# Two of four output-projection pieces multiplied in float32 instead of as rounded parts, and one expert load issued earlier

## The reference, cut to what matters

```python
def _token_mixer(x, w_in, ..., w_out):
    p = _split_columns(x @ w_in)
    ...
    o = jnp.concatenate([o_fox.reshape(B, T, -1), o_nsa.reshape(B, T, -1),
                         o_dsa.reshape(B, T, -1)], axis=-1)
    return o @ w_out            # 1024 x 1024

for l in range(DEPTH):
    mix = _token_mixer(x, ...)
    x = _layer_norm(ALPHA * x + mix, ln1_g[l], ln1_b[l])
    ffn = _moe(x, ...)          # 64 experts, 8 chosen for each token
    x = _layer_norm(ALPHA * x + ffn, ln2_g[l], ln2_b[l])
```

## Time and profile before

| | |
|---|---|
| runs of the kernel before | 1230.63, 1230.74, 1232.79 us; median 1230.74 |
| profiled execution | span 1229.1 us; no other time is recorded for it, so what lies around the span is taken as the distance to the median, 1.6 us |
| PE busy | 1203.0 us (98%) |
| DVE, ACT, POOL busy | 561.5, 347.1, 127.6 us |
| DMA | 454.90 MB, mean 370 GB/s |

### The profile page before, as it was taken

How to read it: one execution, slowest core, us unless ns; L and a number is a source line. 1 busy time by engine, 2 the same in 40 slices (tenths; PEclk the granted TensorE clock), 3 DMA queues, 4 the chain that set the end, 5 groups by cost and what they waited for, 6 DMA issues and landing times.

```text
span 1229.1 us, 25332 instructions
## 1 busy us (share of the span) xinstructions
PE 1203.0 (98%) x10411; PEld 625.6 (51%) x10413; DVE 561.5 (46%) x1554; ACT 347.1 (28%) x717; POOL 127.6 (10%) x173
## 2 busy tenths in 40 slices
PE   9999999999999999999999999999999999999995
PEld 8886843344344343433398868344334443443341
DVE  5888653333333333333388877433333333333334
ACT  5667411111111111111275673111111111111111
POOL 2662200000000000000045431000000000000000
PEclk9999999999999999999999999999999999999999
DMA  9544899999999999999945529999999999999994
GB/s 362 198 175 182 331 408 427 426 426 426 426 427 424 429 426 426 425 427 426 377 168 196 221 106 409 406 427 426 426 428 426 425 427 425 427 426 426 425 428 188
DMA packets 43289, 454.90 MB, mean 370 GB/s; under 512 B 5296, under 2 KB 6064, under 8 KB 8880
## 3 DMA queue, kind: packets, MB, share of 16 engines
q1 hardware_dynamic: 42608, 452.29, 88.5%
q10 hardware_dynamic: 576, 1.05, 0.2%
HBM read 452.27 MB, written 1.05 MB: 369 GB/s over the span
## 4 chain that ended last, share of the span: by engine, by line
PE 79%; DVE 9%; DMA 7%; ACT 3%; issue 1%; POOL 1%; ACTq 0%; DVEq 0%; POOLq 0%
PE banks L1105 34%; PE banks L1132 17%; PE banks L1078 7%; DMA expert_weights<-in_moe_w 5%; PE banks L1143 5%; PE banks L1118 2%; PE banks L1022 1%; PE banks L969 1%; DVE prob L1783 1%; PE banks L1059 1%; PE banks L971 1%; PE banks L970 1%; ACT prob L1380 1%; ACT piece_hi L1307 1%; PE banks L671 1%
## 5 line engine op out<-in xcount | busy, mean ns | idle before, releaser
L1105 PE MATMUL banks<-expert_weights,gathered 128*64 128x512 f32 x1520 | 340.3, 595 | 1.7 <-DMA expert_weights<-in_moe_w 1.7
L1105 PEld LDWEIGHTS banks<-expert_weights,gathered 128*64 128x64 f32 x1520 | 105.2, 137 | 230.0 <-issue 230.0
L1132 PE MATMUL banks<-expert_weights,hT 128*32 128x512 f32 x1600 | 182.0, 595 | 2.3 <-DVE gathered L1972 2.3
L1987 DVE TENSOR_TENSOR sig<-sig,banks 128x256 f32<-128x256 f32 (+1 forms) x66 | 27.2, 413 | 340.9 <-ACT sig L1497 340.9
L1510 ACT ACTIVATE y_hi<-banks,gate_slot 128x512 fp32r<-128x512 f32 x126 | 86.6, 687 | 289.9 <-PE banks L1132 289.9
L1997 DVE SCALAR_TENSOR_TENSOR y_lo<-banks,gate_slot,y_hi 128x512 fp32r<-128x512 f32 x126 | 94.6, 751 | 160.6 <-ACT y_hi L1510 160.6
L1497 ACT ACTIVATE sig<-banks 128x256 f32<-128x256 f32 x64 | 24.6, 384 | 409.9 <-PE banks L1105 409.9
L1078 PEld LDWEIGHTS banks<-hot,x_part 128*128 128x128 bf16 x3072 | 93.3, 98 | 50.3 <-issue 50.3
L1132 PEld LDWEIGHTS banks<-expert_weights,hT 128*32 128x32 f32 x1600 | 47.6, 109 | 108.9 <-issue 108.1
L1078 PE MATMUL banks<-hot,x_part 128*128 128x64 bf16 x3072 | 100.7, 193 | 0.0
L1569 POOL TENSOR_TENSOR piece_lo<-pieces,piece_hi 128x256 fp32r<-128x256 f32 x112 | 90.7, 847 | 72.4 <-ACT piece_hi L1307 58.7
(11 more groups left out here) (262 smaller groups left out, 1527.3 us busy)
## 6 DMA issues: line engine op xcount, KB each, us to landing
expert_weights<-in_moe_w SPq DMA_DIRECT2D x132, 2048.0 KB, 24.2
expert_weights_in_ring<-in_moe_w SPq DMA_DIRECT2D x20, 2048.0 KB, 23.8
pieces<-in_pieces SPq DMA_DIRECT2D x32, 1024.0 KB, 5.8
expert_weights<-in_moe_w SPq DMA_DIRECT2D x26, 1024.0 KB, 9.5
expert_weights_in_rows<-in_moe_w SPq DMA_DIRECT2D x22, 1024.0 KB, 23.1
expert_weights_in_x<-in_moe_w SPq DMA_DIRECT2D x22, 1024.0 KB, 23.9
expert_weights_in_ring<-in_moe_w SPq DMA_DIRECT2D x8, 1024.0 KB, 9.7
shared_weights<-in_ws SPq DMA_DIRECT2D x2, 3072.0 KB, 12.2
```

The costliest lines, as they stand in the source:

```text
L1105: mm = pe.matmul(C[e * PAIR:(e + 1) * PAIR, :], xgT[:, d, e * PAIR:(e + 1) * PAIR], w[e][:, part], start=(d == 0), stop=(d == KD - 1))
L1132: mm = pe.matmul((A, B)[c][to:to + SLOTS, :], hT[:, f, of_:of_ + SLOTS], W[QUARTERS + c][e][:, f * 512:(f + 1) * 512], start=(f == 0), sto ...
```

## The change

Pieces 2 and 3 of the output projection are no longer split. `SPLIT` loses them, so ACT drops three casts and DVE four subtractions a layer. PE multiplies them as float32 weights straight from the ring with float32 activations `xT`, one product in place of three, and waits for `o_sb` (the heads copied to `xT`) where it waited for `heads_split` (their parts made by POOL). Since the `hi` slots of pieces 2 and 3 are then free after the last input projection, load 5 is issued there; at `mix` 3, when nothing reads `x_hi`, `x_lo` and the parts any more, SP now issues both first quarters, load 4 and load 6.

```diff
-SPLIT_OUT = [n for n, (what, c) in enumerate(STREAM) if what == "out"]
+OUT_AT = [n for n, (what, c) in enumerate(STREAM) if what == "out"]
+SPLIT_OUT, WHOLE_OUT = OUT_AT[:2], OUT_AT[2:]
...
-LO_VECTOR = (1, 2, 3, 6, 14, 15, 16)
+LO_VECTOR = (1, 2, 3, 6, 14)
...
                     sp.wait_ge(*at(proj, 2 * N_IN_PIECES))
                     load_half(3, 0)
+                    load(5)
...
                     sp.wait_ge(*at(mix, 2 * TT - 1))
-                    load_first_quarter(0)
+                    for e in range(2):
+                        load_first_quarter(e)
                     load(4)
+                    load(6)
                     sp.wait_ge(*at(mix, 2 * TT))
-                    load_first_quarter(1)
                     load_half(3, 1)
-                    load(5)
-                    load(6)
...
+                        if c == 1:
+                            whole = pair_of(WHOLE_OUT[0], ring)
+                            for k in ks:
+                                mm = pe.matmul(out_, xT[:, k, cols], whole[:, :, k, :], start=(k == 0), stop=(k == KD - 1), skip_group_check=True)
+                            return mm
...
-                        pe.wait_ge(*at(heads_split, k + 1))
+                        if c == 0:
+                            pe.wait_ge(*at(heads_split, k + 1))
...
+                        else:
+                            pe.wait_ge(*at(o_sb, k + 1))
...
-                    split_hi(SPLIT_OUT[2])
...
-                    split_last_hi(0)
...
-                        if v == 6:
-                            split_last_hi(1)
...
-                        if 5 <= u < 9:
-                            split_out(2 + (u - 5) // 2, (u - 5) % 2)
-                        if u in (6, 8):
-                            own.settle()
-                            dve.nop().then_inc(lo_dve, 1)
```

More of the change, by code:

```diff
@@ L37 @@
 LAST_IN_SLOT = STREAM.index(("in", 10)) % RING
-assert LAST_IN_SLOT not in [n % RING for n in SPLIT_OUT]
-LO_VECTOR = (1, 2, 3, 6, 14, 15, 16)
+assert LAST_IN_SLOT not in [n % RING for n in OUT_AT]
+LO_VECTOR = (1, 2, 3, 6, 14)
 LO_POOL = [n for n in SPLIT if n not in LO_VECTOR]
@@ L394, in hi_free, with pair_of @@
                 eng.wait_ge(*at(proj, 2 * c + 2))
-        def lo_pair(n):
+        def pair_of(n, slots):
             a, b = sorted((PLACE_IN_RING[n % RING], PLACE_IN_RING[(n + 1) % RING]))
             assert a == PLACE_IN_RING[n % RING]
-            return lo_ring[:, a:b + 1:b - a]
+            return slots[:, a:b + 1:b - a]
         def flat_piece(t):
@@ L964, in out_product @@
                         cols = slice(t * P, (t + 1) * P)
-                        first = SPLIT_OUT[2 * c]
-                        hi, lo = hi_ring[:, hi_slot(first):hi_slot(first) + 2], lo_pair(first)
                         out_ = mixed_out(t, c).rearrange("p (n c) -> p n c", n=2)
+                        if c == 1:
[3 more added lines that the diff above has]
+                            return mm
+                        hi, lo = hi_ring[:, hi_slot(SPLIT_OUT[0]):hi_slot(SPLIT_OUT[0]) + 2], pair_of(SPLIT_OUT[0], lo_ring)
                         for k in ks:
@@ L975, in out_early @@
                     def out_early(c, k):
-                        pe.wait_ge(*at(heads_split, k + 1))
-                        if k == 0:
-                            for n in (2 * c, 2 * c + 1):
-                                parts_ready(pe, SPLIT_OUT[n])
+                        if c == 0:
+                            pe.wait_ge(*at(heads_split, k + 1))
+                            if k == 0:
+                                for n in SPLIT_OUT:
+                                    parts_ready(pe, n)
+                        else:
+                            pe.wait_ge(*at(o_sb, k + 1))
+                            if k == 0:
+                                for n in WHOLE_OUT:
+                                    pe.wait_ge(*at(piece_ld[n % RING], piece_count(n)))
                         return out_product(0, c, (k,))
@@ L1307, in split_hi @@
                             act.copy(flat_piece(hi_of(n))[:, cols], flat_piece(piece[n % RING])[:, cols]).then_inc(hi_ready, 1)
[L1309 to L1314, removed]
-                            own.settle()
-                            act.nop().then_inc(hi_ready, 1)
                     def columns_out(g):
@@ L1834, in cmp_norm @@
                         V.tensor_tensor(rows_, rows_, pcs[:, 2, :].unsqueeze(2).broadcast_to([P, TT * heads, NC]), ALU.mult).then_inc(pc_ready, 1)
-                    def split_out(i, half):
-                        n, cols = SPLIT_OUT[i], slice(half * SLOT // 8, (half + 1) * SLOT // 8)
-                        dve.wait_ge(*at(hi_ready, SPLIT.index(n) + 2))
-                        own.mark(V.tensor_tensor(flat_piece(piece_lo[n % RING])[:, cols], flat_piece(piece[n % RING])[:, cols],
-                                                 flat_piece(hi_of(n)).bitcast(F32)[:, cols], ALU.subtract))
                     normalise(2)
```

1 line of the change is left out of this document (removed).

## The result

| | before | after |
|---|---|---|
| median of 20 runs each (lowest to highest), us | 1230.59 (1228.74 to 1232.79) | 1233.16 (1231.52 to 1234.97) |
| ratio after / before, 95% interval | | 1.0023 [1.0017, 1.0029]: 2.8 us slower, 2.1 to 3.6 |
| span of the profiled execution, us | 1229.1 | 1232.7 |
| PE busy, us | 1203.0 | 1208.0 |
| DVE, ACT, POOL busy, us | 561.5, 347.1, 127.6 | 552.2, 339.2, 122.4 |

The change costs 2.8 us. The forecast was 1230.4 us and no change that can be measured. The rows show first what came as forecast.

The account below looks back on a forecast made before the run. PE and the chains feeding it were taken as the bound, weight waits costing only 3.5 us. Products (+2.9) less stalls (-1.3) shift PE 1.6 us a layer, mostly swallowed: -0.3 us together, 1230.4 us, range 1228.2 to 1233.4.

Parts of the forecast that it names:

- the products: Output projection on PE: sixteen products a layer go from three rounded records to one float32 product, adding 2.9 us a layer.
- the subtractions: Attention turns: without DVE's four subtractions a layer, three PE stalls of 0.20, 0.86 and 0.27 us go, saving 1.3 us.
- S: Shift of PE's first expert product, later being plus: 2.9 - 1.3 = 1.6 us in both layers.
- A delay of PE of up to 1.9 us is swallowed by waits that vanish: Layer 0's end: PE's waits for weights in the last two pairs absorb a later PE start, up to 1.9 us.
- g: Time by which the stream of expert weights ends earlier through the early load 5: 1 us, between 0 and 3.8.
- the larger of S - 1.9 and -g: How much later layer 0 ends (S - 1.6 in layer 1): -0.3 us in layer 0, 0 in layer 1.
- P: The prediction's account: the weight stream keeps its own time, so layer-end waits soak up a PE delay of up to 1.9 us.
- the queue behind g: Loads on the DMAs before the change: 5.4 us of work still queued when the first refill was issued at 162.39.
- S from 0.6 to 2.9: Likeliest case: time stays within 0.2% whatever g is, from 1228.7 to 1233.0 us; chance 0.72.
- The slower rival: Float32 products cost 0.91 us each and the attention's loop gives nothing back: 3.7 us slower, 1234.4 us; chance 0.13.
- The early load does nothing: Rival on load 5's move: g = 0, S costs at most 0.3 us, 1230.7 to 1231.1 us; chance 0.15 within 0.72.
- That the stream decides: Rival: the stream of weights sets the time, so 4.9 us a layer come back, 9.8 us, giving 1220.9 us; chance 0.02.

Follow-up runs that it names:

- the products alone: Kernel before with its splitting and load order kept, but the sixteen c = 1 products made once in float32 from the lo parts; 1.0055 [1.0041, 1.0068], 6.8 us slower.
- The delay alone: Kernel before plus eight products of zeros on PE ahead of tile 1's c = 1 in each layer; 1.0044 [1.0029, 1.0060], 5.4 us slower.
- the two slices less: Changed kernel with slices k = 5 and 6 of tile 1's c = 1 left out; 0.9996 [0.9987, 1.0005] against the kernel before, 3.8 us less than the changed kernel.

## Why the prediction was wrong

**Right: the products.** 0.43 us a record, 0.86 a product, +2.9 us a layer forecast; +2.8 by the refill of the kernel with the products alone, whose time is 6.8 us longer [5.0, 8.4] for 5.8 of added work. The bound of 0.91 us did not come true.

**Right: the subtractions.** 1.3 us a layer was counted from three stalls. They are all but gone, the refill comes 1.2 us sooner without the subtractions, and the time falls by 2.2 us [1.1, 3.3] for 2.6 forecast.

**Right: S.** 1.6 us forecast; 1.6 in both layers, and the same in all four traces of the changed program with its full work (66.92 to 66.96 us from half load to refill).

**Wrong, and this is the step that failed: "A delay of PE of up to 1.9 us is swallowed by waits that vanish".** It took the stream of weights for a process with its own time, and the end waits for slack. But no further load could be issued until PE had used half of load 0, as the prediction's own paragraph on the loads says. That sentence was used for g alone, which was kept between 0 and 3.8 whatever S is. With it, the stream's end is first use plus a constant, and g falls by one for every unit that S grows. The rule "the larger of S - 1.9 and -g" then holds with g = -1.6 in place of +1, and the layer ends later by S. The sum is 2 x 1.6 = 3.2 us: 1230.6 + 3.2 = 1233.8, against 1233.16 measured. The delay alone (+5.4 us [3.6, 7.4] where P allows 0.3), the two slices less (-3.8 for 3.4 of work), and the distance that stays near 436 us while the start moves, show it.

**Wrong: the queue behind g.** g was put at 1 us from a queue of 5.4 us, read as the landing of the last load ahead of the refill (167.8) less the time of the refill's issue (162.39). What the DMAs had moved by then shows 2.5 us. The 1.06 MB of that queue are the size of one half load; it landed only 5.4 us later, when refills issued from 162.39 on were under way as well. In the changed kernel the same load, issued at 154.84 when the queue was nearly dry, lands after 6.4 us in place of 14.8, and the standstill forecast at 1 to 3 us is one of about 5. Even 2.5 us of queue would have covered a refill 1.6 us later, and it didn't: the lead is spent in the 16 us behind the first refill (24.50 MB moved before and 24.38 in the changed kernel by then), when rooms come free one half at a time. Loads in the old and in the new order give the same time (1.0030 and 1.0027), so the early load is worth 0 within about 2 us for both layers together.

**A small slip in the range.** "S from 0.6 to 2.9 ... whatever g is, from 1228.7" holds for g = 1. With g of 1.3 or more, S = 0.6 gives 1230.74 - 2.3 = 1228.4.

**The rivals.** The measured 1233.16 lies near the upper edge of the range and below its bound of 1233.4. That is luck: the edge was worked out for a larger S with the rule that failed, and S was 1.6. The slower rival was given for S = 3.6; the time went its side by another mechanism: nothing is swallowed. "The early load does nothing" was true, but its time (at most 0.3 us more) was worked out with the same faulty rule. That the stream decides was given 2 in 100 and a gain; in truth the stream does decide the layer's end, but its start is PE's.

**What stays open.** In the fixed window from 165 to 185 us the stream runs at 354 GB/s in the changed kernel, 367 in the old order with float32 products, and 403 before. That window cuts each kernel at another distance from its refill; 30 us behind its own first refill each has moved 30.2 to 30.5 MB. But from 8.64 to 16 us behind the refill the DMAs move only 367 GB/s before and 329 now, with halves already issued, and I have not shown why. Nor is it shown why the delay alone costs more than its 3.5 us. The shift of layer 1's last product in single traces (+3.97) is larger than twice S; the 20 runs say 2.8 [2.1, 3.6], and the scatter of single traces is 0.7 us a layer.

## What to carry to other kernels

A wait at the end of a stage is slack only if what is waited for started on its own; follow the late transfer back through its buffers to the event that released the first of them. When all buffers are spoken for at the consumer's first use, and the stream behind it is the slower of the two, a delay of that first use goes through one for one, and here an earlier prefetch only made a queue into a standstill. And three rounded products were cheaper than one float32 product on PE (0.68 us against 0.86), so parts that other engines make in idle time are worth keeping until they hold PE for longer than the difference.

## What the runs showed of the hardware

A float32 product of 128 x 128 by 128 x 512 takes 0.86 us (two records 0.43 us apart), a rounded one 0.2265, so 3.8 to 1. The Trainium skill (FP8 and Floating Point Precision, TensorE Precision Notes) says that true FP32 takes four passes; the ratio agrees nearly, and a pass took 0.215 us, 5% less than a rounded product.

POOL's subtractions doubled the time of DVE's products of two tensors in SBUF, from 0.51 to 1.02 us each (the rows of 93.14 and 93.74 above). The Trainium skill (GPSIMD Engine Reference, Key points) says that POOL shares its SBUF interfaces with DVE and contends with DVE instructions that have two SBUF inputs; the rows agree, and give the size for this shape.
